# A hybrid decoder layer in float32: five k-tile pairs in seven-product form in the first FFN matmul

## The reference

```python
def swiglu_ffn(x, w_in, w_out):
    gate, up = jnp.split(x @ w_in, 2, axis=-1)
    return (jax.nn.silu(gate) * up) @ w_out

x = x + 0.5 * swiglu_ffn(rmsnorm(x, ffn1_norm[l]), ffn1_w_in[l], ffn1_w_out[l])
...                                     # token mixer
x = x + 0.5 * swiglu_ffn(rmsnorm(x, ffn2_norm[l]), ffn2_w_in[l], ffn2_w_out[l])
```

## Time and profile before

| | |
|---|---|
| median of 3 runs | 1764.4 us |
| the profiled execution, its own time | 1763.82 us |
| its span, first to last instruction | 1762.0 us |
| TensorE busy | 1755.3 us (100% of the span), 8036 matmuls |
| VectorE busy | 1408.5 us (80%) |
| ScalarE busy | 1074.9 us (61%) |
| GpSimd busy | 62.7 us (4%) |
| DMA | 391.75 MB, mean 222 GB/s |
| granted TensorE clock | 1.000 |

### The profile page before, as it was taken

One profiled execution on the slowest core, in us unless ns is written; L12 is line 12 of the kernel. 1 busy time (PEld: TensorE's weight loads), 2 busy tenths in 40 slices (PEclk: granted clock), 3 DMA queues, 4 the chain that ended last, 5 costly groups with the idle time before them and its releaser, 6 DMA issues.

```text
span 1762.0 us, 20916 instructions
## 1 busy us (share of the span) xinstructions
PE 1755.3 (100%) x8036; PEld 1463.3 (83%) x8036; DVE 1408.5 (80%) x1587; ACT 1074.9 (61%) x1359; POOL 62.7 (4%) x74
## 2 busy tenths in 40 slices
PE   9999999999999999999999999999999999999999
PEld 7788888888988888888888888888888888988887
DVE  7888888887899998575655655888888888799998
ACT  7566666666666666554545544666666666666665
POOL 0000000000000001100000000000000000000000
PEclk9999999999999999999999999999999999999999
DMA  9888788876654556555455547687788887764762
GB/s 378 272 261 260 251 250 249 252 252 201 217 215 184 210 215 208 178 193 177 160 188 163 173 168 262 169 256 244 249 260 260 260 261 240 226 204 166 259 213 90
DMA packets 160691, 391.75 MB, mean 222 GB/s; under 512 B 6504, under 2 KB 15232, under 8 KB 155856
## 3 DMA queue, kind: packets, MB, share of 16 engines
q1 hardware_dynamic: 152288, 342.02, 54.7%
q0 software_dynamic: 7184, 46.42, 12.6%
q10 hardware_dynamic: 1120, 1.97, 0.3%
HBM read 347.37 MB, written 3.69 MB: 199 GB/s over the span
## 4 chain that ended last, share of the span: by engine, by line
PE 95%; DVE 2%; DMA 1%; SPq 1%; issue 1%; ACT 0%; POOL 0%; ACTq 0%; POOLq 0%; DVEq 0%
PE bank L584 9%; PE bank L582 9%; PE bank L583 9%; PE bank L566 7%; PE bank L568 7%; PE bank L567 7%; PE bank L523 7%; PE bank L525 7%; PE bank L524 6%; PE bank L653 5%; PE bank L655 5%; PE bank L654 5%; PE bank L679 3%; PE bank L681 3%; PE bank L680 3%; PE bank L551 1%
## 5 line engine op out<-in xcount | busy, mean ns | idle before, releaser
L1188 DVE TENSOR_TENSOR wlo<-raw,whi 128x1024 fp32r<-128x1024 f32 (+1 forms) x586 | 696.6, 1207 | 224.7 <-ACT whi L849 222.0
L849 ACT ACTIVATE whi<-raw 128x1024 fp32r<-128x1024 f32 (+1 forms) x586 | 611.0, 1047 | 390.2 <-PE bank L525 189.2
L582 PE MATMUL bank<-whi,xs 128*128 128x512 f32 (+1 forms) x768 | 297.9, 388 | 0.4 <-DVE xs L1370 0.2
L584 PE MATMUL bank<-whi,xs 128*128 128x512 f32 (+1 forms) x768 | 295.6, 385 | 0.0
L583 PE MATMUL bank<-wlo,xs 128*128 128x512 f32 (+1 forms) x768 | 295.5, 385 | 0.0
L1188 DVE TENSOR_TENSOR wlo<-tsum,whi 128x1024 fp32r<-128x1024 f32 (+1 forms) x120 | 140.2, 1196 | 60.5 <-ACT whi L849 60.5
L849 ACT ACTIVATE whi<-tsum 128x1024 fp32r<-128x1024 f32 (+1 forms) x120 | 122.2, 1036 | 103.9 <-PE bank L584 64.1
L582 PEld LDWEIGHTS bank<-whi,xs 128*128 128x128 f32 x768 | 144.4, 188 | 29.0 <-issue 0.9
L584 PEld LDWEIGHTS bank<-whi,xs 128*128 128x128 f32 x768 | 144.3, 188 | 27.7
L583 PEld LDWEIGHTS bank<-wlo,xs 128*128 128x128 f32 x768 | 144.4, 188 | 26.8
L653 PE MATMUL bank<-whi,aw_hi 128*128 128x512 f32 x420 | 164.0, 391 | 0.0
(11 more groups left out here) (203 smaller groups left out, 2670.4 us busy)
## 6 DMA issues: line engine op xcount, KB each, us to landing
raw<-ffn_w_in SPq DMA_DIRECT2D x158, 1024.0 KB, 7.1
raw<-ffn_w_out SPq DMA_DIRECT2D x84, 1024.0 KB, 6.5
raw<-w_in SPq DMA_DIRECT2D x48, 1024.0 KB, 5.1
tsum<-raw POOLq DMA_DIRECT2D x36, 1024.0 KB, 7.2
raw<-w_out SPq DMA_DIRECT2D x16, 1024.0 KB, 4.9
raw<-ffn_w_in SPq DMA_DIRECT2D x16, 768.0 KB, 4.6
tsum<-raw POOLq DMA_DIRECT2D x4, 768.0 KB, 5.7
x<-x SPq DMA_DIRECT2D x4, 512.0 KB, 12.4
```

Of the source, the lines that this page charges most:

```text
L582: mm(banks[b][:, 0:w], xs[:, k + i, 0, tok], hi, start=starts[b] and k + i == 0, stop=False, skip_group_check=True)
L584: last = mm(banks[b][:, 0:w], xs[:, k + i, 1, tok], hi, start=False, stop=k + i == last_k, skip_group_check=True)
L849: A(whi[:, h % SLOTS, 0:n_el], src, ACT.Copy).then_inc(weights_hi, 1)
L1188: V.tensor_tensor(wlo[:, h % SLOTS, 0:n_el], src, whi[:, h % SLOTS, 0:n_el].bitcast(f32), ALU.subtract).then_inc(weights_lo, 1)
```

## The change

The k-tiles of units 1 to 10 are divided anew: tiles 0 to 5 plain (three halves for gate, GA, GB, GC, and three for up, UA, UB, UC), tiles 6 to 15 as five pairs in seven-product form. Each form is now three halves, two of 1024 columns and one of 512 (called the mini here; its weights lie in `minis` and `tmini`). Each half, mini or not, takes one of the four slots. A unit is 27 halves and 177 matmuls.

The T2 sum goes from a DMA to VectorE (`sum_t2`), and each sum is two instructions (2048 and 512 columns). T1's sum stays in the unit before, T2's stands after GA, T3's after the first half of B21. T4's sum is made by two adding DMAs, one for the 1 MB and one for the mini.

The new buffers lie where `x` was, so `x` leaves on-chip memory during the units. It is read again from the input (u = 0) or from a copy (`x_kept`, u = 1) when the units end. The copy is stored by GpSimd's queue, behind its `x_power(2)`, and SyncE's queue waits for it ahead of the first mini's load.

```diff
+FORM_K0, FORM_PAIRS = 6, 5
-UNIT_HALVES = 22
+UNIT_HALVES = 27
...
+        place[0] = x_at
+        last_plain = sb("last_plain", [P, 2 * W])
+        minis = sb("minis", [P, FORM_SLOTS, W])
+        tmini = sb("tmini", [P, W])
...
+                if j == 1 and name == "B11":
+                    sp.wait_ge(ss_done, 8 * (2 * u + 1))
+                    if u:
+                        sp.wait_ge(x_psum, 8)
+                        sp.wait_ge(x_stored, 16)
+                sp.dma_start(minis[:, raw_slot(n), 0:w], w_in[:, k + 4, col:col + w]).then_inc(raw_full[raw_slot(n)], 16)
...
             def add_piece(u, j, name, after, done):
+                pool.dma_start(tmini[:, 0:w], minis[:, raw_slot(n), 0:w], accum_op=ALU.add).then_inc(done, 16)
+
+            def x_again(u):
+                pool.wait_ge(weights_lo, OUT[u])
+                pool.dma_start(x[:], (x_kept if u else io["x"][0]).rearrange("(b p) d -> p b d", p=P)).then_inc(x_back, 16)
             for j in range(1, UNITS):
-                add_piece(0, j, "B22", T1, t2_added)
                 add_piece(0, j, "B21", T2, t4_added)
+            x_again(0)
...
             x_power(2)
+            pool.wait_ge(x_updated, 8 * 2)
+            pool.dma_start(x_kept.rearrange("(b p) d -> p b d", p=P), x[:]).then_inc(x_stored, 16)
...
             def form(h, bank_out, stationary, w, start):
-                for i in range(2):
+                for i in range(3):
                     pe.wait_ge(weights_lo, h + i + 1)
                     slot = (h + i) % SLOTS
-                    for k in range(2):
+                    for k in range(2 if i < 2 else 1):
...
+            def last_form_split(u):
+                dve.wait_ge(last_hi, u + 1)
+                V.tensor_tensor(last_split(1), last_sums, last_split(0).bitcast(f32), ALU.subtract).then_inc(last_ready, 1)
...
+            def sum_t2(u, j):
+                n22, w = unit_piece(u, j, "B22"), UNIT_W[j]
+                full(n22)
+                dve.wait_ge(weights_lo, unit_half(u, j) + T1 + 3)
+                V.tensor_tensor(tsum[:, 0:4 * w], raw[:, raw_slot(n22), 0:4 * w], tsum[:, 0:4 * w], ALU.add)
+                V.tensor_tensor(tmini[:, 0:w], minis[:, raw_slot(n22), 0:w], tmini[:, 0:w], ALU.add).then_inc(sums_done, 1)
...
+                for i in range(3):
+                    form_split(T1, i)
+                form_split(B11, 0, "B11")
                 swiglu(u, j - 1)
+                for i in range(1, 3):
+                    form_split(B11, i, "B11")
+                plain_split("GA", GA)
+                sum_t2(u, j)
+                plain_split("GB", GB)
+                for i in range(3):
+                    form_split(T2, i)
+                form_split(B21, 0, "B21")
+                sum_t3(u, j)
+                for i in range(1, 3):
+                    form_split(B21, i, "B21")
```

More of the change, by code:

```diff
@@ L166, in sb @@
             return t
+        x_at = place[0]
         x = sb("x", [P, TB, D_MODEL])
+        x_end = place[0]
         xs_at = place[0]
@@ L364, in piece @@
             def piece(n, src, tiles, w):
                 slot = raw_slot(n)
[L366 to L369, removed]
+                wait_free(n)
                 sp.dma_start(raw[:, slot, 0:tiles * w].rearrange("p (k f) -> p k f", k=tiles), src).then_inc(raw_full[slot], 16)
@@ L993, in unit @@
+                act_e.wait_ge(sums_done, 3 * first + 1)
+                for i in range(3):
+                    form_split(T1, i)
+                loaded(unit_piece(u, j, "B11"))
+                for i in range(3):
+                    form_split(B11, i, "B11")
+                plain_split("GA", GA)
+                act_e.wait_ge(weights_used, base + T1 + 3)
                 A(gset[:, s, 1, 0:w], Z[:, 0:w], ACT.Copy).then_inc(copied, 1)
-                split(base + G0 + 1, piece_half(n + LOAD["G0"], 1, w2), w2)
@@ L995, in unit @@
-                act_e.wait_ge(weights_used, base + B11 + 2)
+                plain_split("GB", GB)
+                act_e.wait_ge(weights_used, base + B11 + 3)
                 act_e.wait_ge(act_f_done, 2 * (UNITS * u + j))
                 A(p1s[:, 0:w], Y[:, 0:w], ACT.Copy).then_inc(copied, 1)
-                act_e.wait_ge(t2_added, 16 * (first + 1))
-                for i in range(2):
-                    split(base + T2 + i, tsum[:, i * w2:(i + 1) * w2], w2)
-                loaded(n + LOAD["B21"])
@@ L1002, in unit @@
-                for i in range(2):
-                    split(base + B21 + i, piece_half(n + LOAD["B21"], i, w2), w2)
-                act_e.wait_ge(sums_done, 2 * first + 2)
-                split(base + T3, piece_half(n + LOAD["B12"], 0, w2), w2)
-                act_e.wait_ge(weights_used, base + T2 + 2)
-                A(gset[:, s, 0, 0:w], Y[:, 0:w], ACT.Copy).then_inc(copied, 1)
-                split(base + T3 + 1, piece_half(n + LOAD["B12"], 1, w2), w2)
-                loaded(n + LOAD["G1"])
@@ L1020, in unit @@
-                for i in range(2):
-                    split(base + U0 + i, piece_half(n + LOAD["U0"], i, w2), w2)
-                loaded(n + LOAD["U1"])
-                split(base + U1, piece_half(n + LOAD["U1"], 0, w2), w2)
+                act_e.wait_ge(sums_done, 3 * first + 2)
+                for i in range(3):
+                    form_split(T2, i)
+                loaded(unit_piece(u, j, "B21"))
+                for i in range(3):
+                    form_split(B21, i, "B21")
+                act_e.wait_ge(sums_done, 3 * first + 3)
@@ new lines, in unit @@
+                form_split(T3, 0, "B12")
+                act_e.wait_ge(weights_used, base + T2 + 3)
+                A(gset[:, s, 0, 0:w], Y[:, 0:w], ACT.Copy).then_inc(copied, 1)
+                for i in range(1, 3):
+                    form_split(T3, i, "B12")
+                plain_split("GC", GC)
+                loaded(unit_piece(u, j, "B22"))
+                for i in range(3):
+                    form_split(B22, i, "B22")
+                act_copy(u, j - 1)
+                act_e.wait_ge(t4_added, 32 * (first + 1))
@@ L1024, in unit @@
+                for i in range(3):
+                    form_split(T4, i)
+                plain_split("UA", UA)
+                plain_split("UB", UB)
                 silu(u, j)
-                split(base + U1 + 1, piece_half(n + LOAD["U1"], 1, w2), w2)
+                plain_split("UC", UC)
             def ffn_out(u):
```

289 lines of the change are left out of this document (175 added, 114 removed).

## The result

The changed kernel takes 1845.56 us (median of 4 runs, 1845.54 to 1845.99) against 1764.25 us before on the same chip (4 runs, 1763.71 to 1764.69). The ratio is 1.0462, with a 95% interval of 1.0443 to 1.048: slower by 81 us. The forecast was 1845, its range 1825 to 1860.

The account below looks back on a forecast made before the run. TensorE's matmuls were taken as the bound. Full units 57.6 us, last units 6.5, first units 2.4 and 2.9, the store 10.7: 80.5 on 1763.8, plus 0.6 for the median, gives 1845 us; range 1825 to 1860.

Parts of the forecast that it names:

- the places: Four points in a unit (swiglu and the sums of T2, T3, T1) where long VectorE jobs may starve TensorE; 4.30 us with restarts.
- The unit: A full unit: 41.02 us of TensorE work plus 4.30 of waits and restarts, 45.3 us, 3.6 more than 41.70.
- B11's second half: Swiglu between B11's first and second split: TensorE has 4.76 us of work against 5.84, so waits 1.08 us.
- B21's second half: T3's sum between B21's first and second split: TensorE has 4.76 us of work against 6.59, so waits 1.83 us.
- UB: T1's sum ahead of UB's split: TensorE has 9.52 us of work against 10.65, so waits 1.13 us.
- T2's sum: Between the splits of GA and GB: 7.03 us against TensorE's 7.01, a wait of 0.02 us, just hidden.
- rival B: Only throughput counts: VectorE's 42.5 us a unit sets the time, 0.8 more than before, 1791 us; chance 0.07.
- Rival A: VectorE's 39.1 us fit in 41.0 and a unit's waits stay under 0.68 us: 1761, or 1750 us; chance 0.08.
- The last units and the first ones: Last units 3.2 us more each, with waits of 1.57, 1.65 and 0.29; first units 2.4 and 2.9 more.
- The store: Start of part 2: loads queue behind the store of x, taken as 9 us; TensorE waits 10.7 us before T1.
- rival C: The forecast, plus the clock falling after the store's wait: T1's 15 matmuls cost 3.4 us more, 1848; chance 0.20.
- Rival D: T4's second adding DMA comes late on one queue beside loads: 1 us a unit, 1865 us; chance 0.05.

Follow-up runs that it names:

- E2: The changed kernel with T3's sum moved earlier, between T1's second and third split, VectorE's work unchanged; 1810.57 us.
- E3: The changed kernel with swiglu moved behind GA's split, T2's sum up behind T1's splits and the transposes behind GA; 1828.45 us.
- E4: The changed kernel with T1's sum one split later, behind UB instead of UA; 1826.34 us.
- E5: The changed kernel with T2's sum given back to adding DMAs, 2.8 us less VectorE work per unit; 1851.0 us.
- E7: The changed kernel with an unused 1024-column VectorE reduction (1.13 us) added in each unit ahead of T1's third split; 1847.45 us.
- E6: The changed kernel with each sum cut into three parts at separate places, swiglu behind GA, transposes behind T2, x stored before the scale; 1760.18 us.
- E1: The changed kernel with GpSimd storing x ahead of the scale instead of behind it; 1836.74 us.
- E8: The changed kernel with an unused 1024-column VectorE reduction added in each unit behind T3's sum, ahead of B21's second split; 1899.54 us.

## Why the prediction was right

The bound, the places and the sum were as forecast. That the total came within 1 us is in part luck: errors cancelled at the store, and smaller ones in the units.

**The unit:** forecast 45.3, measured 45.45. The three waits, each with the 0.16: B11's second half 1.05 (forecast 1.08), B21's second half 1.81 (1.83), UB 1.08 (1.13). T2's sum shows no wait (0.02). The three and their restarts, 0.11 each, make 4.27 of the 4.43 us above 41.02; the rest is some twenty steps a little over 0.23. E2, E3 and E4 each removed one of them and gave back 1.95, 1.16 and 1.18 a unit, the wait and its restart, as the working had them.

**That load does not decide,** rival B and the load side of A: refuted by E2 (same work, 35 us less), E5 (2.8 us less work per unit, no gain), E7 (1.1 us more work per unit, no loss in a steady unit) and E6. Rival A's point, waits under 0.68 us a unit, is reached only by E6, whose unit is 0.25 above TensorE's own 41.02.

**The last units and the first ones:** part 1 came to 34.05 where the terms give 34.4. The waits of a last unit were 1.24 and 1.35 by the rows (1.40 and 1.51 from start to start) for 1.57 and 1.65, and the third, 0.29 at UA, did not come. Unit 9 was forecast as a full one, 3.6 more, and was 3.1, since its wait ahead of UB was only 0.26. Units 2 to 8, at 3.75 or a little more for 3.6, made up for most of that.

**The store:** a wait of 10.7 was forecast, and 8.17 (8.3 with the 0.16) came. The mis-sized term is the transfer: I put it at 9 us between bounds of 5.2 and 12.4, and it landed in 6.7. (In E1 and E6, beside other transfers, it took 11.5, near the other bound.)

```profile
x_kept<-x POOLq DMA_DIRECT2D x1, 2048.0 KB, 6.7
```

**The clock:** the forecast had it not fall, rival C had it fall. It fell: 13 matmuls at 0.43 cost 13 x 0.2 = 2.6 us where C said 3.4. So the case that I gave 0.60 was wrong in this step, and C, at 0.20, was right in mechanism. 8.3 and 2.6 make 10.9, and 10.7 was in the sum: the total hid both errors. E1, which takes both away, shortens that stretch by 54.32 - 43.66 = 10.7. By the rule of the Trainium skill ("TensorE: Matmul & The Clock Gate", Why this matters for your kernels) a long gap brings the lower level; the trace agrees, with 0.50 behind the 8.17 us. C should have had more than half.

**Rival D:** nothing. No wait of TensorE is put down to a DMA, and the unit with both halves of T4 on one queue is within 0.15 of the forecast. Its adding DMAs took 6.9 and 7.6 us.

**What was missing:** 1.9 us in the last stretch, forecast 0. There are one wait of 0.26 us and twenty steps of about 0.3 us where 0.23 is due, seven before, in its first 85 us. VectorE has no slack there (58.8 of 60 us busy in the changed kernel, 58.9 before), and after the last unit it once waits 3.1 us for ScalarE:

```profile
DVE wlo L1298 <- ACT whi L951: 4.4, 2, 3.1
```

The same stretch of part 1 lost nothing (213.25 us for 213.22), and no run took it apart: the cause stays open.

## What to carry to other kernels

An added job that fits into an engine's free time can still cost its whole length. Count, from the moment at which a slot comes free, everything that must pass through each engine before the next half is ready, against what TensorE has ready in that time; a job costs what stands over. Where it stands over, move it, or cut it and put the parts behind long halves, before any work is taken away: moving one uncut sum was worth 35 us here and all of E6 85 us, while giving one sum back to a DMA made the kernel 5 us slower.

## What the runs showed of the hardware

The granted clock can fall behind a short wait, and the same wait does not always do it. Behind 1.65 us (17 times in the changed kernel, 83 times in E1, E3, E4, E5 and E7) it never fell. Behind 1.93 it fell in E1, E3 and E5 and did not in E4 and E7, nor in the changed kernel itself, where the same unit has the same wait:

```profile
391.18 0.50 PE L667 MATMUL bank<-whi,xs 128*128 128x512 f32 x1 [1.93 <-DVE wlo L1298]
391.51 0.39 PE L668 MATMUL bank<-wlo,xs 128*128 128x512 f32 x1
391.74 0.40 PE L669 MATMUL bank<-whi,xs 128*128 128x512 f32 x1
```

Behind 2.12 (E3) and 3.37 (E5) it fell, behind 2.21, twice in E8, it did not, and behind 2.77 to 3.06 it fell in E8 17 times out of 18. In E8 the fall began at any point from 0.64 us before the restart to 1.12 after it (1.41 in E3), and cost 1.4 to 1.7 us in 13 cases and 3.0 in four. So a job of 1.13 us cost 2.7 us a unit, where one expects 1.13. What decides whether the clock falls, no run here shows.

The wait of 1.93 us is 0.28 longer than its neighbours, in each of these kernels in the same unit. In the changed kernel ScalarE starts B21's first high part 0.54 us after TensorE's first matmul of T2 and not 0.26 (384.86 for 384.32, against 248.24 for 247.98):

```profile
384.86 2.08 ACT L951 ACTIVATE whi<-raw 128x1024 fp32r<-128x1024 f32 x2 [2.04 <-PE bank L685]
```

That is the 0.28. Why ScalarE starts later there was not found.
